# The first modulation moved from a stage of its own into the input projection, and an attention product in two column halves

## The reference, cut to what matters

```python
c_act = jax.nn.silu(c)                      # c: (1, 1024)
mod = c_act @ w_ada[l] + b_ada[l]           # w_ada: (1024, 6144)
shift1, scale1, gate1, shift2, scale2, gate2 = jnp.split(mod, 6, axis=-1)
h = layer_norm(x) * (1.0 + scale1) + shift1     # x: (1024 tokens, 1024)
proj = h @ w_in[l]                              # 6416 columns
...
p = jnp.exp(s - m)                              # sliding window, 16 heads of 64
p = p / (jnp.sum(p, -1, keepdims=True) + jnp.exp(sink - m))
o = jnp.einsum('bkgnqj,bnjkd->bnqkgd', p.astype(v.dtype), vb)
```

## Time and profile before

| | |
|---|---|
| median of 3 runs | 4884.5 us |
| the profiled execution, its own time | 4883.0 us |
| its span | 4881.3 us |
| start, 0 to 10 us; ada0, to about 58 us | first matmul at 20.87 us |
| g_in, from about 58 us | first matmul of the projection at 83.55 us |
| attention woven in | about 228 to 820 us |
| PE busy over the span | 4150.2 us (85%) |
| DVE busy over the span | 2600.9 us (53%) |

### The profile page before, as it was taken

The page is one execution under the profiler, slowest core; times in us unless marked ns, Lnnn a source line. Parts: engine busy times, 40 slices in busy tenths (PEclk is TensorE's granted clock), DMA queues, the critical chain, the costliest instruction groups (busy, mean ns, idle before and its releaser), DMA issues. The chain is left out here.

```text
span 4881.3 us, 74471 instructions
## 1 busy us (share of the span) xinstructions
PE 4150.2 (85%) x28954; PEld 3446.2 (71%) x28954; DVE 2600.9 (53%) x4866; ACT 1489.8 (31%) x3127; POOL 685.9 (14%) x774
## 2 busy tenths in 40 slices
PE   5999999767899999599995576798875799989978
PEld 3899888556688877499995332687764699965646
DVE  3567775565333348611106687677764325646745
ACT  2233232643222235311103233233433311133423
POOL 1111111221000000000002102000012114423321
PEclk8999999778899999799997678799987899999998
DMA  4444432441211134412212465444434334553334
GB/s 160 159 145 144 139 129 87 179 155 65 57 52 43 43 117 162 144 67 84 78 54 96 145 244 215 115 116 109 131 84 138 123 105 172 183 155 96 99 100 138
DMA packets 430694, 589.34 MB, mean 121 GB/s; under 512 B 166297, under 2 KB 317202, under 8 KB 428772
## 3 DMA queue, kind: packets, MB, share of 16 engines
q1 hardware_dynamic: 382425, 418.15, 27.9%
q0 software_dynamic: 46336, 164.57, 9.0%
q10 hardware_dynamic: 1616, 2.36, 0.1%
HBM read 429.41 MB, written 155.57 MB: 120 GB/s over the span
## 5 line engine op out<-in xcount | busy, mean ns | idle before, releaser
L320 PE MATMUL g_in_g_acc<-g_in_g_whi,g_in_hi 128*128 128x444 f32 (+4 forms) x960 | 357.1, 372 | 14.9 <-DVE g_in_g_wlo L310 9.9
L321 PE MATMUL g_in_g_acc<-g_in_g_wlo,g_in_hi 128*128 128x444 f32 (+4 forms) x960 | 346.3, 361 | 0.0
L322 PE MATMUL g_in_g_acc<-g_in_g_whi,g_in_lo 128*128 128x444 f32 (+4 forms) x960 | 345.6, 360 | 0.0
L196 PE MATMUL g_even_acc<-g_even_w_hi,h_hi 128*128 128x384 f32 (+1 forms) x960 | 317.2, 330 | 19.4 <-DVE g_even_w_lo L238 19.4
L198 PE MATMUL g_even_acc<-g_even_w_lo,h_hi 128*128 128x384 f32 (+1 forms) x960 | 317.1, 330 | 0.0
L199 PE MATMUL g_even_acc<-g_even_w_hi,h_lo 128*128 128x384 f32 (+1 forms) x960 | 316.9, 330 | 0.0
L320 PE MATMUL g_odd_g_acc<-g_odd_g_whi,h_hi 128*128 128x344 f32 (+3 forms) x816 | 264.0, 324 | 30.8 <-DVE g_odd_g_wlo L310 17.0
L321 PE MATMUL g_odd_g_acc<-g_odd_g_wlo,h_hi 128*128 128x344 f32 (+3 forms) x816 | 262.3, 321 | 0.0
L1597 DVE SCALAR_TENSOR_TENSOR up_cv<-up_acc,up_taps,up_cv 128x1023 f32<-128x1023 f32 x88 | 112.8, 1282 | 280.2 <-ACT up_cv L1573 273.0
L322 PE MATMUL g_odd_g_acc<-g_odd_g_whi,h_lo 128*128 128x344 f32 (+3 forms) x816 | 261.7, 321 | 0.0
L214 DVE COPY g_even_o_buf<-g_even_acc 128x384 f32<-128x384 f32 (+1 forms) x60 | 32.1, 535 | 399.0 <-PE g_even_acc L199 399.0
(11 more groups left out here) (579 smaller groups left out, 9987.2 us busy)
## 6 DMA issues: line engine op xcount, KB each, us to landing
down_raw<-in_w_down SPq DMA_DIRECT2D x66, 512.0 KB
g_in_m_w<-in_ada_w SPq DMA_DIRECT2D x24, 1024.0 KB, 5.4
up_w_buf<-in_w_up SPq DMA_DIRECT2D x44, 512.0 KB
U2p<-g_even_o_buf POOLq DMA_DIRECT2D x11, 1920.0 KB, 7.8
g_odd_x<-U3p SPq DMA_DIRECT2D x24, 768.0 KB
g_even_w_buf<-in_even_w_in SPq DMA_DIRECT2D x11, 1536.0 KB
g_in_m_w<-in_w_ada SPq DMA_DIRECT2D x16, 1024.0 KB, 6.2
prep_near<-U2p SPq DMA_DIRECT2D x18, 896.0 KB
```

Source lines behind the costliest of these rows:

```text
L196: mm = pe.matmul(o, hi[:, k, tt], w_hi[:, par, k, :wd], start=k == 0, stop=not split and k == kc - 1)
L320: pe.matmul(bank[:, :wd], hi[:, k, tt], w_hi[:, st % 2, k, :wd], start=k == 0, stop=False)
L321: pe.matmul(bank[:, :wd], hi[:, k, tt], w_lo[:, st % 2, k, :wd], start=False, stop=False)
L322: op = pe.matmul(bank[:, :wd], lo[:, k, tt], w_hi[:, st % 2, k, :wd], start=False, stop=k == KC - 1)
```

## The change

The stages start and ada0 go. What they did is done inside g_in:

- `w_ada`'s first 2048 columns are loaded in eight slices of 1 MB (128 rows of 8 KB), one for each k, into `first_w`, 64 KB in each partition. `first_w` lies where `hi` and `lo` will lie afterwards, so no slice waits for a buffer. SP issues slices 0 to 3, chunks 0 to 3 of `w_in`, and slices 4 to 7, without a wait.
- c is loaded by ACT's queue and its silu is written 32 times side by side (`c_wide`, 128x32 for each k). For each slice four matmuls (`row_sum`) are issued, one for each 512 columns, and the four go to four groups of 32 partitions of one PSUM bank: 32x512 each, at columns 0, 32, 64 and 96 of the array. So one instruction on DVE copies all 2048 sums, four transposes turn them, and two small instructions add the bias and the 1.
- PE does slices 0 to 3, then the transposes of the first token tile and of the bias, then slices 4 to 7 and the four transposes. The sums no longer go through HBM.
- The identity, the bias rows and the zero rows of `U2p` and `U3p` are transferred by ACT's queue. POOL's constants wait for the first `in_T`.
- In `weigh` each matmul is split in two: 64 columns of the probabilities give 64 partitions of the output. 16 matmuls stand where 8 stood.

```diff
+            def load_first(k):
+                sp.dma_start(first_w[:, k], w_first.rearrange("(p k) n -> p k n", k=KC)[:, k]).then_inc(first_in[k], DMA)
...
-            sp.dma_start(shift_scale_rows[:], shift_scale.rearrange("(r p) -> r p", p=P)).then_inc(s.rows_in, DMA)
-            for c in range(KC + RAW):
+            for k in range(KC):
+                load_first(k)
+                if k == KC // 2 - 1:
+                    for c in range(RAW):
+                        gemm.load(sp, c)
+            for c in range(RAW, KC + RAW):
                 gemm.load(sp, c)
...
             load_in(0)
             load_in(1)
+            pool.wait_ge(s.in_T, 1)
...
-                    pe.matmul(po[:, h, :], pT[:, q % 2, 2 * slot, :], vv[:, 1 - t % 2, kv * SHD:(kv + 1) * SHD], start=True, stop=False)
-                    op = pe.matmul(po[:, h, :], pT[:, q % 2, 2 * slot + 1, :], vv[:, t % 2, kv * SHD:(kv + 1) * SHD], start=False, stop=True)
+                    for side, par in ((0, 1 - t % 2), (1, t % 2)):
+                        for to in (slice(0, SHD), slice(SHD, P)):
+                            op = pe.matmul(po[to, h, :], pT[:, q % 2, 2 * slot + side, to], vv[:, par, kv * SHD:(kv + 1) * SHD], start=side == 0, stop=side == 1)
...
+            def row_sum(k):
+                pe.wait_ge(first_in[k], DMA)
+                for n in range(4):
+                    op = pe.matmul(row_sums[32 * n:32 * n + 32], c_wide[:, k], first_w[:, k, n * 512:(n + 1) * 512], start=k == 0, stop=k == KC - 1)
+                if k == KC - 1:
+                    op.then_inc(s.row_mm, 1)
...
+            act.dma_start(c_first[:], conds[0].rearrange("(p k a) -> p k a", k=KC, a=1), allow_slow_non_contiguous=True).then_inc(s.c_in, DMA)
+            act.dma_start(bias_rows[:], b_first.rearrange("(r p) -> r p", p=P)).then_inc(s.rows_in, DMA)
+            act.dma_start(ident[:], t_eye).then_inc(s.id_in, DMA)
+            act.wait_ge(s.c_in, DMA)
+            act.activation(c_wide, c_first[:].broadcast_to([P, KC, 32]), ACT.Silu).then_inc(s.c_silu, 1)
...
             def turn_in(t):
                 if t == 0:
+                    dve.wait_ge(s.row_mm, 1)
+                    dve.tensor_copy(rows_out, row_sums).then_inc(s.rows, 1)
                     dve.wait_ge(s.cols_T, 1)
-                    flat = pm[:].rearrange("p a c -> p (a c)")
-                    dve.tensor_copy(cols[:, 0:KC], flat[:, 0:KC])
-                    dve.tensor_scalar(cols[:, KC:], flat[:, KC:2 * KC], 1.0, None, ALU.add)
+                    by_chunk = cols[:].rearrange("p (n b) -> p n b", b=4)
+                    dve.tensor_tensor(by_chunk[:, 0:2], rows_T[:, 0:2], by_chunk[:, 0:2], ALU.add)
+                    dve.scalar_tensor_tensor(by_chunk[:, 2:], rows_T[:, 2:], 1.0, by_chunk[:, 2:], ALU.add, ALU.add)
...
+                if t == 1:
+                    dve.wait_ge(s.bias_T, 1)
+                    dve.tensor_copy(cols[:], bias_T)
                 norm(t)
...
-def start_stage(nc, ident, t_eye, padded):
...
-        start_stage(nc, ident, T["t_eye"], (U2p, U3p))
-        ada_stage(nc, [([T["c"][0]], T["w_ada"][0][:, 0:2 * D], T["b_ada"][0][0:2 * D], mod1[:, 0:2 * D])])
```

More of the change, by code:

```diff
@@ L57, in col_view @@
     return vec.rearrange("(k p) -> p k", p=P)
[L60 to L119, removed]
@@ L1031, with in_stage @@
 SWA_FROM = QB_STRIPS * NT
-def in_stage(nc, ident, src, shift_scale, w_in, P1, pos, sinks, t_mask, t_first, t_freq, YB, conds, mods):
-    with stage(nc, "g_in", "cond", "silu", "rows_in", "cols_T", "cols", "in_even", "in_odd", "var", "std", "xn", "in_T", "h", "h_hi", "h_lo",
+def in_stage(nc, ident, t_eye, padded, src, w_first, b_first, w_in, P1, pos, sinks, t_mask, t_first, t_freq, YB, conds, mods):
+    with stage(nc, "g_in", "id_in", "zero", "pad_out", "c_in", "c_silu", "f0", "f1", "f2", "f3", "f4", "f5", "f6", "f7", "bias_T", "row_mm", "rows", "cond", "silu", "rows_in", "cols_T", "cols", "in_even", "in_odd", "var", "std", "xn", "in_T", "h", "h_hi", "h_lo",
                "m_even", "m_odd", "mb0", "mb1", "mb2", "mb3", "m_acc", "m_mm", "m_res", "m_out_even", "m_out_odd", "const", "init", "arg", "table", "x_even", "x_odd", "roped", "turned", "qkT", "scores", "s_free",
@@ L1043, in in_stage @@
         G = 4
+        with nc.sbuf_tensor("g_in_first", [P, KC, 2 * D], F32) as first_w:
+            pass
         hi = sb("hi", [P, KC, SEQ], F32R)
@@ L1072, in in_stage @@
         y = sb("y", [P, SH, SHD])
-        shift_scale_rows = sb("shift_scale_rows", [2 * KC, P])
+        bias_rows = sb("bias_rows", [2 * KC, P])
+        c_first = sb("c_first", [P, KC, 1])
         cols = sb("cols", [P, 2 * KC])
@@ L1091, in in_stage @@
         xn, h = pT[:, 0].rearrange("p c t -> p (c t)"), pT[:, 1]
+        first_in = (s.f0, s.f1, s.f2, s.f3, s.f4, s.f5, s.f6, s.f7)
+        row_sums = pm[:].rearrange("p a c -> p (a c)")
+        c_wide = x[:, 0, 512:512 + KC * 32].rearrange("p (k m) -> p k m", m=32)
+        rows_out = x[:, 1, 0:512]
+        rows_T = pS[:].rearrange("p a c -> p (a c)")[:, 0:512].rearrange("p (b n q) -> p n b q", n=4, q=32)[:, :, :, 0]
+        bias_T = po[:].rearrange("p a d -> p (a d)")[:, 0:2 * KC]
+        zeros = x[:, 0, 0:P]
         def in_order(norm, turn_in, unit, step, mod):
@@ L1119, in _ @@
         def _(sp):
+            def load_first(k):
+                sp.dma_start(first_w[:, k], w_first.rearrange("(p k) n -> p k n", k=KC)[:, k]).then_inc(first_in[k], DMA)
             def load_x(t):
+                if t == 0:
+                    sp.wait_ge(s.pad_out, 2 * len(padded) * DMA)
                 if t >= 2:
@@ L1250, in step @@
                     score(t, n // 2)
-            def turn_in(t):
+            def row_sum(k):
[4 more added lines that the diff above has]
+                    op.then_inc(s.row_mm, 1)
+            def turn_in(t):
+                if t == 0:
+                    pe.wait_ge(s.c_silu, 1)
+                    for k in range(KC // 2):
+                        row_sum(k)
+                    pe.wait_ge(s.id_in, DMA)
                 pe.wait_ge(s.xn, t + 1)
[L1254 to L1257, removed]
+                if t:
                     pe.wait_ge(s.h, t)
@@ L1261, in turn_in @@
                 op.then_inc(s.in_T, 1)
+                if t == 0:
+                    pe.wait_ge(s.rows_in, DMA)
+                    pe.transpose(bias_T, bias_rows[:], ident[:2 * KC, :2 * KC]).then_inc(s.bias_T, 1)
+                    for k in range(KC // 2, KC):
+                        row_sum(k)
+                    pe.wait_ge(s.rows, 1)
+                    for b in range(4):
+                        op = pe.transpose(pS[:].rearrange("p a c -> p (a c)")[:, b * P:(b + 1) * P], rows_out[:, b * P:(b + 1) * P], ident[:])
+                    op.then_inc(s.cols_T, 1)
             def unit(u):
@@ L1281, in _ @@
         def _(act):
+            act.dma_start(c_first[:], conds[0].rearrange("(p k a) -> p k a", k=KC, a=1), allow_slow_non_contiguous=True).then_inc(s.c_in, DMA)
[3 more added lines that the diff above has]
+            act.activation(c_wide, c_first[:].broadcast_to([P, KC, 32]), ACT.Silu).then_inc(s.c_silu, 1)
+            act.wait_ge(s.zero, 1)
+            for t in padded:
+                for row in (0, t.shape[0] - 1):
+                    act.dma_start(t[row].rearrange("(q c) -> q c", c=P), zeros[0:t.shape[1] // P]).then_inc(s.pad_out, DMA)
             def expose(t, g):
@@ L1490, in first @@
             def first(t):
+                if t == 0:
+                    dve.memset(zeros, 0.0).then_inc(s.zero, 1)
+                if t == 1:
+                    dve.wait_ge(s.bias_T, 1)
+                    dve.tensor_copy(cols[:], bias_T)
                 norm(t)
@@ L4025, in tables @@
     }
-def start_stage(nc, ident, t_eye, padded):
[L4030 to L4035, removed]
-        @block.sync
-        def _(sp):
-            sp.dma_start(ident[:], t_eye).then_inc(s.id_in, DMA)
-            sp.wait_ge(s.zero, 1)
-            for t in padded:
-                for row in (0, t.shape[0] - 1):
-                    sp.dma_start(t[row:row + 1, :], zero[:, :t.shape[1]]).then_inc(s.pad_out, DMA)
-            sp.wait_ge(s.id_in, DMA)
-            sp.wait_ge(s.pad_out, 2 * len(padded) * DMA)
 @contextmanager
```

2 lines of the change are left out of this document (1 added, 1 removed).

## The result

The changed kernel takes 4829.14 us, the median of four runs (4823.43 to 4837.14), against 4882.56 us before; the ratio is 0.9896, with a 95% interval of 0.9882 to 0.9910. That is 53.4 us less (44 to 58 by the interval). Measured again later beside the other experiments, it was 4830.53 against 4884.01 us, ratio 0.9889 (0.9873 to 0.9905). The profiled execution has a span of 4821.8 us, its own time is 4823.4 us.

What follows compares the result with a forecast made beforehand. It took the opening as bound by transfers, matmuls and HBM in series, the attention by PE; 37.5 us (opening) plus 19 us (value product) off 4883.0 gave 4826.5, plus 1.5 for the median, said as 4827; range 4812 to 4845 us.

Steps and rivals of the forecast that it cites:

- The value product: Attention: 1.17 us per product instead of 1.83, 21 us over 32 products, 19 us after 2 us taken off.
- the chain behind the low parts: Opening, from DVE's last low part to the first projection matmul: 2.5 + 5.4 us, so 38.1 becomes 46.0.
- The end of the low parts: Opening: last slice landed at 34.5 us, chunk 4 0.6 later, DVE's low parts 2.9 more, so 38.1 us.
- the unbroken block above 350 GB/s: Sign of being right, in the opening: one unbroken DMA block above 350 GB/s from 3 to 34 us.
- The four sums: Opening, PE's four matmuls per slice: side by side, 0.9 to 1.7 us a slice, ending at 36.2, ahead of DVE.
- the other end: Opening, worst case: sums one after another, 3.5 us a slice, 6.9 slow; end at 38.4, 0.3 us behind DVE.
- What DVE might take back: Attention: 2 us off the products' 21 us, since DVE, just in time for a strip before, may be late.
- The sum: Whole kernel: 37.5 us from the opening plus 19 from the value product, 56.5 us off, forecast 4827 us.
- DVE did not take over: Rival, attention: DVE instead of PE paces the steps, the 19 us do not arrive, 4840.5 us; chance 0.10.
- the sums do not follow each other: Rival, opening: the four sums run one by one at the slow price, 4841 us; chance 0.05.
- the transfers were not slow: Rival, opening: transfers slow or badly mixed at 300 GB/s, 4835 us; inside the forecast's spread, which has 0.79.
- the halves do overlap: Rival, attention: halves do not overlap, 0.11 us a record, products lose 55.7 us, 4901 us; chance 0.02.

Runs made afterwards that it cites:

- experiment 5: Three kernels, the changed kernel with POOL's constants and third and fourth x tile, constants alone, or those x tiles alone issued after the last sum: 4828.70, 4823.82, 4822.11 us.
- experiment 4: The changed kernel with a slice's four sums all in partitions 0 to 31 of four PSUM banks, collected by four DVE copies: 4833.96 us, one run.
- experiment 3: The changed kernel with all eight matmuls for the first 64 output partitions of a value product ahead of the other eight: ratio to before 0.9940.
- experiment 1: The changed kernel with the value product of before, eight full matmuls, so the new opening alone: ratio to before 0.9940.
- experiment 2: The kernel before with only the value product split in halves: ratio to before 0.9963.
- the kernel with POOL late: The changed kernel with POOL's constants and third and fourth x tile all issued after the last sum: 4828.70 us, one run.

## Why the prediction was right

It said 4827 us and a first matmul at 46.0; measured were 4829.14 us and 45.90. (By its own terms the sum is 4826.5 + 1.5 = 4828.) The value product and the chain behind the low parts were right by themselves. The end of the low parts was right by luck: two errors of about three microseconds cancelled.

- *The end of the low parts*, 38.1 forecast, 38.35 measured (37.23 + 1.12). The rate was taken as 376 GB/s from ada0's strips of 2 KB rows; the 8 KB rows gave about 420, and the last slice's sums began at 31.85 instead of behind 34.5, although the transfers of POOL's queue did count, as assumed (without them it is 28.75). But the chunks did not land 0.6 to 2.3 us behind the last slice; ACT took them up 1.8 to 4.8 us behind the start of those sums, since POOL's constants and x tiles were in their way (experiment 5). Counting the two x tiles and the constants by their bytes, and all ahead of the last slice, was the weak step: POOL issued these x tiles at 26.29 us, not from 20 to 25, and they fell among the chunks; and the constants cost about 3 us instead of 0.8 to 0.9. Two of the signs that were named did not come, the unbroken block above 350 GB/s and a last matmul on `first_w` at 35 to 38 us (it ended at 33.8).
- *From there to the first matmul*, 7.9 us forecast, 7.55 measured.
- *The four sums*, taken at 1.7 us a slice, measured 1.93. That the other end was worth next to nothing was right too: experiment 4 shows the serial case at 3.44 us a slice, with the last sum done at about 37.8 us and the copies directly behind the low parts, as before. The 1.24 us by which it is later come from its four copies.
- *The value product*, 1.17 us forecast, 1.17 measured (0.09 in, 1.08 for the rest). Order, form and number of the records were those of the earlier trace rows, and experiment 3 shows that the order had to agree.
- *What DVE might take back*, 2 us. The stretch got 19.25 us shorter, against 21 by the products. But PE's waits for DVE are 10.2 us instead of 9.9, so not what was named. The halves gave 20.0 us against experiment 1 and 21.8 us in experiment 2, so single profiles differ by as much as the missing 2 us, and whether anything was lost is not shown.
- *The sum*, 56.5 us, against 56.9 at the end of the stage in the profile and 53.4 between medians, whose interval (44 to 58) holds it.

The rivals: DVE did not take over; the sums do not follow each other, and where they do (experiment 4) they are fast from 11.4 us on; the transfers were not slow, about 420 GB/s, though they did not mix well: the constants alone cost 3.0 us at the last slice; the halves do overlap. That each later stage would be as long as before held only within the spread of single profiles, up to 9 us for one stage of the same kernel (494.2 and 503.0 us).

## What to carry to other kernels

Before pricing a split into column halves, look for a stream in the same trace with the same form and the same order, and count records from start to start; the halves pay only where neighbours use different columns. When a stage is cut away, follow what is last afterwards: here it is not the big transfer but four small chunks queued behind it, and issuing 0.33 MB of constants behind the x tiles and the last sum was worth 3.5 us at the first matmul. And read a gain of a few us at the end of the stage that is touched: the others differ by as much from one execution to the next.

## What the runs showed of the hardware

- One queue with rows of 8 KB ran at 423 GB/s (20 to 25 us); strips with rows of 2 KB had 376. Within the changed kernel, too, the rate fell to 370 and 376 GB/s from 15.0 to 17.5 us, while the chunks with rows of 1712 bytes came.
- With the small packets of the constants in the queue, the DMA engines were busy for a share of 0.96 while 93 GB/s flowed (30.0 to 31.3 us); with them issued later, and the x tiles earlier, 377 and 356 GB/s flowed from 30.0 to 32.5 us.
- Four 32-column groups with 512 columns each ran beside each other: eight records in 1.93 us, each of them at the lower clock of 1.2 GHz by its length (1060 ns against 592 at the shortest). In that stretch the granted clock reads 1.00, so the column doesn't show this. In experiment 4, where PE did not pause, records became short at 11.4 us. In the kernel with POOL late one slice ran with short records, after transposes on PE: eight of them in 1.07 us, where one group takes 3.44.

```profile
L1215 PE MATMUL g_in_pm<-g_in_first,g_in_x x64: 592/1061/1063, 6.5 to 29.6; 128*32 128x512 f32 x64
21.28 1.07 PE L1215 MATMUL g_in_pm<-g_in_first,g_in_x 128*32 128x512 f32 x8 [1.12 <-DMA g_in_first<-in_w_ada]
```

These are two lines of the kernel with POOL late: shortest, median and longest record in ns, and the short slice on the timeline.
